# Row vectors, squares and clips of the recurrent tiles on other engines, in a fused transformer kernel

## The reference

```python
# RWKV-7, 4 heads of 64
r, k, v, wd, ad, gd = split_cols(hb)
w_log = -softplus(-(w0 + tanh(wd) @ w_up)) - 0.5
decay = exp(-exp(w_log))
a = sigmoid(a0 + ad @ a_up)
g = sigmoid(gd) @ g_up
kk = l2_normalize(heads(k * k_k), 1e-12)
k = k * (1.0 + (a - 1.0) * k_a)
if v_first is None: v_first = v                                  # layer 0
else: v = v + (v_first - v) * sigmoid(v0 + (v @ v_down) @ v_up)  # layer 1
y = rwkv7_scan(r, decay, k, v, -kk, kk * a)

# gated deltanet, 4 heads of 64, in chunks of 64 tokens
q = l2_normalize(heads(q), 1e-6) * 64 ** -0.5
k = l2_normalize(heads(k), 1e-6)
g = cumsum(g within the chunk)
decay[t, s] = exp(g[t] - g[s]) for s <= t, else 0
```

## Time and profile before

| | |
|---|---|
| three runs | 3709.7, 3712.3, 3714.1 us (median 3712.3) |
| the profiled execution, span | 3708.2 us |
| instructions | 55795 |
| TensorE | busy 3610.1 us |
| VectorE | busy 1972.4 us |
| ScalarE | busy 1502.7 us |
| GpSimd | busy 1623.7 us |
| HBM read | 286 MB |

### The profile page before, as it was taken

One profiled execution on the slowest core, in us unless ns is written; L12 is line 12 of the kernel. 1 busy time (PEld: TensorE's weight loads), 2 busy tenths in 40 slices (PEclk: granted clock), 3 DMA queues, 4 the chain that ended last, 5 costly groups with the idle time before them and its releaser, 6 DMA issues.

```text
span 3708.2 us, 55795 instructions
## 1 busy us (share of the span) xinstructions
PE 3610.1 (97%) x23122; PEld 2996.1 (81%) x23122; DVE 1972.4 (53%) x3453; ACT 1502.7 (41%) x2665; POOL 1623.7 (44%) x883
## 2 busy tenths in 40 slices
PE   9999999999899999999999899999999999999999
PEld 8878888888788888888767888888888866788887
DVE  2356554344645544553677745544652496765552
ACT  3444333434433343333555443334333455534332
POOL 3114566421266635664322135664665322225664
PEclk9999999999999999999999999999999999999999
DMA  4103332311243234322210034323332220012332
GB/s 130 40 29 99 112 103 68 89 52 35 69 136 102 63 101 132 103 63 89 74 46 2 3 125 121 103 66 112 103 102 81 83 57 24 3 42 89 99 103 97
DMA packets 393405, 291.95 MB, mean 79 GB/s; under 512 B 17056, under 2 KB 355904, under 8 KB 393152
## 3 DMA queue, kind: packets, MB, share of 16 engines
q1 hardware_dynamic: 387728, 284.49, 25.2%
q10 hardware_dynamic: 5136, 2.70, 0.4%
q0 software_dynamic: 288, 1.18, 0.1%
HBM read 286.24 MB, written 2.10 MB: 78 GB/s over the span
## 4 chain that ended last, share of the span: by engine, by line
PE 83%; DVE 10%; ACT 4%; issue 1%; POOL 1%; ACTq 0%; DMA 0%; DVEq 0%; SPq 0%; POOLq 0%
PE ps L811 13%; PE ps L812 13%; PE ps L813 13%; PE ps L1040 4%; PE ps L1042 4%; PE ps L1041 4%; PE ps L943 3%; PE ps L940 3%; PE ps L942 3%; PE ps L1068 2%; PE ps L1600 2%; PE ps L1088 2%; PE ps L1077 1%; PE ps L1150 1%; PE ps L838 1%
## 5 line engine op out<-in xcount | busy, mean ns | idle before, releaser
L3453 POOL TENSOR_TENSOR wl<-wraw,wh 128x1024 fp32r<-128x1024 f32 (+1 forms) x424 | 1026.4, 2426 | 1553.1 <-ACT wh L2771 1549.6
L811 PE MATMUL ps<-x_T,wh 128*128 128x512 f32 (+1 forms) x2224 | 850.2, 382 | 0.0
L812 PE MATMUL ps<-x_T,wh 128*128 128x512 f32 (+1 forms) x2224 | 849.0, 382 | 0.0
L813 PE MATMUL ps<-x_T,wl 128*128 128x512 f32 (+1 forms) x2224 | 849.0, 382 | 0.0
L2771 ACT ACTIVATE wh<-wraw 128x1024 fp32r<-128x1024 f32 (+1 forms) x424 | 446.0, 1053 | 763.1 <-PE ps L813 489.1
L811 PEld LDWEIGHTS ps<-x_T,wh 128*128 128x128 f32 x2224 | 418.5, 188 | 81.1 <-issue 0.5
L813 PEld LDWEIGHTS ps<-x_T,wl 128*128 128x128 f32 x2224 | 418.4, 188 | 80.6
L812 PEld LDWEIGHTS ps<-x_T,wh 128*128 128x128 f32 x2224 | 418.4, 188 | 80.7 <-issue 0.5
L2048 DVE TENSOR_TENSOR scr<-scr,ps 128x512 f32<-128x512 f32 x132 | 90.7, 687 | 465.3 <-ACT scr L2926 465.3
L1040 PE MATMUL ps<-wh,h_T 128*128 128x512 f32 x672 | 262.5, 391 | 0.4
L1041 PE MATMUL ps<-wl,h_T 128*128 128x512 f32 x672 | 261.5, 389 | 0.0
(11 more groups left out here) (816 smaller groups left out, 6877.6 us busy)
## 6 DMA issues: line engine op xcount, KB each, us to landing
wraw<-in_ffn_w_gate_dram SPq DMA_DIRECT2D x88, 512.0 KB, 3.9
wraw<-in_ffn_w_up_dram SPq DMA_DIRECT2D x88, 512.0 KB, 3.9
wraw<-in_w_in_dram SPq DMA_DIRECT2D x82, 512.0 KB, 3.8
wraw<-in_w_gate_dram SPq DMA_DIRECT2D x44, 512.0 KB, 3.9
wraw<-in_w_up_dram SPq DMA_DIRECT2D x44, 512.0 KB, 3.8
mix<-in_ffn_w_down_dram SPq DMA_DIRECT2D x20, 1024.0 KB, 7.1
arena<-in_ffn_w_down_dram SPq DMA_DIRECT2D x12, 1024.0 KB, 6.2
wraw<-in_ffn_w_down_dram SPq DMA_DIRECT2D x24, 512.0 KB, 3.7
```

The lines of the kernel that those rows point to most:

```text
L811: mm(b[:, t0:t1], wh[:, k, :], xTh[:, k, t0:t1], k == 0, False)
L812: mm(b[:, t0:t1], wh[:, k, :], xTl[:, k, t0:t1], False, False)
L813: ins = mm(b[:, t0:t1], wl[:, k, :], xTh[:, k, t0:t1], False, k == 7)
L3453: tt(wl, raw_of(w), wh.bitcast(F32), ALU.subtract).then_inc(*g.sig("w", "lo", w))
```

## The change

The row vectors w0, v0 and a0 are no longer added by DVE. PE adds each in the bank, by one more product with K = 1: a row of ones times the row vector. The banks' release moves from DVE's signal "ua" to ACT's "sg", since ACT now takes the Sigmoids right from the banks (in layer 1 three of 256 columns instead of one of 256 and one of 512). The square of kk moves from DVE to ACT, behind the other squares and ahead of the load of the Exp table; DVE signals "kk" for it and later does the sum. The square of q is taken with scale 8, which, with an epsilon of 64e-6, replaces the factor 0.125. The epsilons are added by POOL, from a small tile that five memsets fill at the start. The two clips become two Relu's on ACT, the second with scale -1, and both exponentials get scale -1. The tile eps_o is written but not read.

```diff
--- before.py
+++ after.py
@@ -628,6 +628,7 @@
         ind = con[:, C_IND:C_IND + 2]
         omu = sml(54)[:, 0:7]
         half = sml(55)
+        eps_k, eps_o = sml(56), sml(57)
         vf3 = vfirst[:, :].rearrange("p (t n) -> p t n", t=4)
 
         def c64(n, k=1):
@@ -1459,18 +1460,22 @@
                     ins.then_inc(*S("tin", n))
                 yield
                 KB, BK, tmp = get(), get(), get()
-                b1, f1 = bank(K("lw"), K("ua"))
-                b2, f2 = bank(K("la"), K("ua"))
+                b1, f1 = bank(K("lw"), K("sg"))
+                b2, f2 = bank(K("la"), K("sg"))
                 b3, f3 = bank(K("lg"), K("GG"))
                 pe.wait_ge(*f1)
                 pe.wait_ge(*at("lora", l))
-                ins = mm(b1[:, 0:256], hbT[0:32, 6, js], lora[0:32, :], True, True)
+                pe.wait_ge(*at("pb2", l))
+                mm(b1[:, 0:256], hbT[0:32, 6, js], lora[0:32, :], True, False)
+                ins = mm(b1[:, 0:256], ones[0:1, :], rows["w0"][0:1, :], False, True)
                 if l:
                     pe.wait_ge(*at("rec", "vz", l))
-                    ins = mm(b1[:, 256:512], vz[0:32, js], vup[0:32, :], True, True)
+                    mm(b1[:, 256:512], vz[0:32, js], vup[0:32, :], True, False)
+                    ins = mm(b1[:, 256:512], ones[0:1, :], rows["v0"][0:1, :], False, True)
                 ins.then_inc(*S("b1"))
                 pe.wait_ge(*f2)
-                mm(b2[:, 0:256], hbT[32:64, 6, js], lora[32:64, :], True, True).then_inc(*S("b2"))
+                mm(b2[:, 0:256], hbT[32:64, 6, js], lora[32:64, :], True, False)
+                mm(b2[:, 0:256], ones[32:33, :], rows["a0"][32:33, :], False, True).then_inc(*S("b2"))
                 pe.wait_ge(*f3)
                 mm(b3[:, 0:256], hbT[64:128, 6, js], lora[64:128, :], True, True).then_inc(*S("b3"))
                 yield
@@ -2492,27 +2497,20 @@
                 GG = K3[:, 256:512]
                 yield
                 KB, BK, tmp = get(), get(), get()
-                b1, b2 = psum_of(*K("lw")), psum_of(*K("la"))
-                v.wait_ge(*at(*K("b1")))
-                tt(LW[:, 0:256], b1[:, 0:256], rows["w0"], ALU.add)
-                if l:
-                    tt(UA[:, 256:512], b1[:, 256:512], rows["v0"], ALU.add)
-                v.wait_ge(*at(*K("b2")))
-                tt(UA[:, 0:256], b2[:, 0:256], rows["a0"], ALU.add).then_inc(*S("ua"))
                 yield
                 r_, k_, v_ = RK[:, 0:256], RK[:, 256:512], VV[:, 0:256]
                 a_ = UA[:, 0:256]
                 kk = KB[:, 0:256]
                 nn = sml(j)
                 v.wait_ge(*at(*K("in", 0)))
-                step(tt(kk, k_, rows["k_k"], ALU.mult))
-                step(tt(tmp[:, 0:256], kk, kk, ALU.mult))
-                red(nn[:, 0:4], h64(tmp[:, 0:256], 4), op=ALU.add).then_inc(*S("kk2"))
+                v.wait_ge(*at("pb2", l))
+                tt(kk, k_, rows["k_k"], ALU.mult).then_inc(*S("kk"))
                 yield
                 v.wait_ge(*at(*K("q2")))
-                step(red(nn[:, 4:12], h64(BK, 8), op=ALU.add))
-                ts(nn[:, 0:4], nn[:, 0:4], 1e-12, None, ALU.add)
-                ts(nn[:, 4:12], nn[:, 4:12], 1e-6, None, ALU.add).then_inc(*S("nn"))
+                red(nn[:, 4:12], h64(BK, 8), op=ALU.add)
+                v.wait_ge(*at(*K("kk2")))
+                red(nn[:, 0:4], h64(tmp[:, 0:256], 4), op=ALU.add).then_inc(*S("nn"))
+                v.wait_ge(*v.own())
                 yield
                 v.wait_ge(*at(*K("sg")))
                 step(stt(tmp[:, 0:256], a_, 1.0, rows["k_a"], ALU.subtract, ALU.mult))
@@ -2531,7 +2529,6 @@
                 bcb = bc(gb_[:, j, :].unsqueeze(2), [P, 4, 64])
                 v.wait_ge(*at("rec", "gb", l))
                 v.wait_ge(*at(*K("nroot")))
-                step(ts(nn[:, 4:8], nn[:, 4:8], 0.125, None, ALU.mult))
                 tt(h64(kk, 4), h64(kk, 4), bc(nn[:, 0:4].unsqueeze(2), [P, 4, 64]), ALU.mult)
                 step(tt(h64(QK, 8), h64(QK, 8), bc(nn[:, 4:12].unsqueeze(2), [P, 8, 64]), ALU.mult), *K("QK"))
                 tt(BK[:, 0:256], kk, a_, ALU.mult)
@@ -2567,9 +2564,8 @@
                 RW = [get(), get()]
                 DT, DN = DTN[:, 0:256], DTN[:, 256:512]
                 v.wait_ge(*at(*K("gd")))
-                step(tt(v4(DT), v4(psum_of(*K("gd"))[:, 0:256]), bc(gcs[:, 0:4].unsqueeze(2), [P, 4, 64]), ALU.subtract))
-                step(ts(DN, DT, 0.0, None, ALU.max))
-                ts(DT, DT, 0.0, None, ALU.min).then_inc(*S("DN0"))
+                tt(v4(DT), v4(psum_of(*K("gd"))[:, 0:256]), bc(gcs[:, 0:4].unsqueeze(2), [P, 4, 64]),
+                   ALU.subtract).then_inc(*S("DN0"))
                 yield
                 for par in range(2):
                     if par:
@@ -3232,12 +3228,17 @@
                 nn = sml(j)
                 s.wait_ge(*at("rec", "gg", l))
                 copy(h64(LW[:, 256:512], 4), bc(gg[:, j, :].unsqueeze(2), [P, 4, 64]))
-                s.wait_ge(*at(*K("ua")))
-                act(LW[:, 0:256], LW[:, 0:256], ACT.Sigmoid)
-                w_ = 512 if l else 256
-                act(UA[:, 0:w_], UA[:, 0:w_], ACT.Sigmoid).then_inc(*S("sg"))
+                s.wait_ge(*at(*K("b1")))
+                act(LW[:, 0:256], psum_of(*K("lw"))[:, 0:256], ACT.Sigmoid)
+                if l:
+                    act(UA[:, 256:512], psum_of(*K("lw"))[:, 256:512], ACT.Sigmoid)
+                s.wait_ge(*at(*K("b2")))
+                act(UA[:, 0:256], psum_of(*K("la"))[:, 0:256], ACT.Sigmoid).then_inc(*S("sg"))
                 s.wait_ge(*at(*K("in", 2)))
-                act(BK, QK, ACT.Square).then_inc(*S("q2"))
+                act(BK[:, 0:256], QK[:, 0:256], ACT.Square, scale=8.0)
+                act(BK[:, 256:512], QK[:, 256:512], ACT.Square).then_inc(*S("q2"))
+                s.wait_ge(*at(*K("kk")))
+                act(tmp[:, 0:256], KB[:, 0:256], ACT.Square).then_inc(*S("kk2"))
                 if j:
                     s.preload_act_table(ACT.Exp)
                 yield
@@ -3287,7 +3288,10 @@
                 RW = [get(), get()]
                 yield
                 s.wait_ge(*at(*K("DN0")))
-                act(DTN[:, 0:256], DTN[:, 0:256], ACT.Exp)
+                act(DTN[:, 256:512], DTN[:, 0:256], ACT.Relu).then_inc(*s.sig("step"))
+                s.wait_ge(*s.own())
+                step(act(DTN[:, 0:256], DTN[:, 0:256], ACT.Relu, scale=-1.0))
+                act(DTN[:, 0:256], DTN[:, 0:256], ACT.Exp, scale=-1.0)
                 act(DTN[:, 256:512], DTN[:, 256:512], ACT.Exp, scale=-1.0).then_inc(*S("DN"))
                 if 0 < j < 3:
                     s.preload_act_table(ACT.Sigmoid)
@@ -3492,6 +3496,8 @@
                 yield
                 nn = sml(j)
                 g.wait_ge(*at(*K("nn")))
+                tt(nn[:, 0:12], nn[:, 0:12], eps_k[:, 0:12], ALU.add).then_inc(*S("neps"))
+                g.wait_ge(*g.own())
                 tt(nn[:, 0:12], nn[:, 0:12], half[:, 0:12], ALU.pow).then_inc(*S("nroot"))
                 yield
                 E1, E3X, E4 = get(), get(), get()
@@ -3626,6 +3632,11 @@
                 use(ENDS, True)
                 stage(wat[0] + AHEAD)
 
+            g.memset(eps_k[:, 0:4], 1e-12)
+            g.memset(eps_k[:, 4:8], 64e-6)
+            g.memset(eps_k[:, 8:12], 1e-6)
+            g.memset(eps_o[:, 0:4], 64e-5)
+            g.memset(eps_o[:, 4:8], 1e-6)
             g.memset(half[:, 0:12], -0.5).then_inc(*g.sig("half", 0))
             g.wait_ge(*at("half", 0))
             g.wait_ge(*at("w0", 0))
```

## The result

The changed kernel took 3721.24 us in the median of 7 runs (3717.14 to 3728.70); the kernel before 3711.16 us in 7 runs beside it. The ratio is 1.0026, with a 95% interval of 1.0016 to 1.0035: slower, by 10 us. I had said 3719.9 us, with 0.44 on slower and 0.45 on no measurable difference. The spans of the two profiled executions are 3708.2 and 3719.4 us.

A forecast was written before the change was run, and what follows sets the result against it. In the tiles PE and DVE hand work to each other, neither alone the bound. Layer 0's 2.93 us and layer 1's 4.68 us made +7.6 us on the 3712.3 us median: 3719.9 us, range 3707 to 3729.

The forecast's parts named there:

- The products: Products with ones on PE in each tile's front: +0.63 us in layer 0, +1.06 us in layer 1.
- The square ahead of the table load: ACT squares kk before loading Exp; second solve level in tiles 2 and 3 later by 1.03 us, layer 1 1.46.
- The factor 0.125: DVE's L2534 leaves the path in tiles 2 and 3: -0.20 us in layer 0, -0.35 us in layer 1.
- The clips: L2571 and L2572 leave DVE for two Relu's on ACT; removed time becomes wait: 0, up to 0.25 us.
- The table load's drain: Skill page's drain of about 1380 ns would add some 5.5 us over four tiles; forecast followed the trace, without drain.
- POOL's add: Epsilon add on POOL before the pow: 0.3 us taken, bounds 0.1 and 2.3; on the path in layer 0's tile 1.
- Tile 1: Second tile of each layer: +0.54 us in layer 0, +1.3 us in layer 1, the latter the least certain term.
- Tile 0: First tile of each layer, front beside attention: +0.73 us in layer 0, +1.16 us in layer 1.
- rival C: New idle before the solve's level lowers TensorE's clock, 3.0 us per stretch; 3729 us if three or more tiles; chance 0.14.
- A: DVE is the true bound in the tiles; its removed time, 19 us, comes off: 3693 us; chance 0.09 with half-way forms.
- B: Wait for kk does not bite at the second solve level; idle hides the products: 3710 to 3713 us; chance 0.22.

The follow-up runs named there:

- e1: Kernel before with only the products with ones moved to TensorE: median 3719.3 us, ratio 1.0021, +5.7 us against the kernel before at an equal clock.
- e4: Changed kernel without the products with ones, VectorE adding the row vectors again: 3711.7 us, ratio 0.9996 to the kernel before, -0.4 us at an equal clock.
- e7: Changed kernel with each product with ones issued twice: 3738.4 us, ratio 1.0070 to the kernel before, +16.5 us at an equal clock.
- e8: Kernel before with seven useless products filling TensorE's idle time before L1515 in tiles 2 and 3: 3712.5 us, ratio 1.0001.
- e10: Changed kernel with products of 32 rows of ones instead of one (results wrong, only times used): 3717.1 us, ratio 1.0011 to the kernel before.
- e3: Changed kernel with the Exp table load put ahead of ScalarE's wait for kk and its square: 3723.3 us, ratio 1.0027 to the kernel before.
- e2: Kernel before with only the square of kk on ScalarE, ahead of the Exp table load, its sum moved later: 3712.4 us, ratio 1.0001.

## Why the prediction was right, point by point

**The products: right in kind, too dear in layer 0, and their cover did not exist as an extra.** I took 0.63 and 1.06 us; it is 0.44 (2067.53 - 2066.46 against 0.63) and 0.98 (from 1.06 to 2.04 in layer 1, L1469 at 3241.68 to L1480 at 3243.72). I let the 0.63 us idle swallow the products and then charged the same delay again through the late kk: of the +1.03 us at the second level 0.63 is the products and 0.40 the square. That way of counting hid the main thing: the removal of L2509 and L2510 from before L2645 pays for the wait for ScalarE, and the products are on the path in full. e1 (+5.7), e4 (-0.4) and e7 show that.

**The square ahead of the table load: right in mechanism, mis-sized.** I took 0.40 us for it, beside the products' 0.63. The wait is 0.85 us in all four tiles, but what it adds from kk's start to c1 is 0.15, since the level ran 2.19 us before, beside the end of the u product, and 2.01 now, alone. With the products' 0.44 this is 0.59 against my 1.03; in layer 1 1.13 against 1.46. The slack of 1.3 us in the prediction is that behind the first of the two copies; behind both it was 1.0 (2066.99 + 0.76 = 2067.75, to 2068.76).

**The factor 0.125: right in layer 0, too large in layer 1.** I took 0.20 and 0.35 off. From c1 to PE's next wait for DVE it was 10.90 (2070.95 to 2081.85) and is 10.70 (L1489 at 2080.31 to L1520 at 2091.01): 0.20. In layer 1 it was 0.20 too, not 0.35 (11.07 before, 10.87 after, from 3253.46 to 3264.33):

```profile
2084.24 0.42 DVE L2641 TENSOR_TENSOR arena<-arena,ps 128x256 f32<-128x256 f32 x1 [1.99 <-PE ps L1701]
2084.70 0.43 DVE L2532 TENSOR_TENSOR spare<-spare,small 128x256 f32<-128x256 f32 x1
```

**The clips: right.** They cost and bring nothing. DVE, which had waited 0.66 us in the earlier trace rows, now waits twice, 0.28 and 0.73 us:

```profile
2100.16 0.69 DVE L2575 TENSOR_TENSOR scr<-ps,cr 128x512 f32<-128x512 f32 x1 [0.28 <-PE ps L1566]
2101.59 0.76 DVE L2613 COPY_PREDICATED arena<-cr,ps 128x512 f32<-128x512 int32 x1 [0.73 <-PE ps L1605]
```

**The table load's drain.** By the Trainium skill ("ScalarE: Activation LUTs", What ACT_TABLE_LOAD costs) a switch of tables costs a drain of about 1380 ns on top of the load. In the changed kernel the copy starts at 2077.86, 0.01 us after the load's end at 2077.85. The row decides. An estimate by the page's figure would have put the sum about 5.5 us higher than the forecast.

**POOL's add: right.** I took 0.3 with its wait; L3499 lasts 0.21 and the power starts 0.29 us after it in tile 1, 0.36 and 0.44 in tile 3.

```profile
2008.28 0.21 POOL L3499 TENSOR_TENSOR small<-small 128x12 f32<-128x12 f32 x1 [40.28 <-DVE small L2512]
2008.57 2.27 POOL L3501 TENSOR_TENSOR small<-small 128x12 f32<-128x12 f32 x1
```

**Tile 1: right in layer 0.** 37.65 to 38.23 us at full clock, +0.58 against my 0.54 (the products alone 0.36 in e1, all the rest 0.22 in e4); in layer 1 39.14 to 40.15, +1.01 against 1.3.

**Tile 0: too dear in layer 0.** I took +0.73 us. From the attention product (L1077, L1078) that waits 0.34 us shortly ahead of this front to the tile's first mask copy, e8, which has the kernel before's tile 0, and e10 have windows at full clock:

```profile
1941.26:1984.68 43.42, 42.37 (x308) 30.43 (x308) 32.28 (x111) 26.83 (x74) 9.23 (x8) 1.00 0.00 1
1938.77:1982.34 43.57, 42.83 (x312) 30.85 (x312) 29.79 (x103) 28.00 (x78) 9.67 (x9) 1.00 0.00 1
```

It is +0.15 (43.59 in e3, +0.17). In layer 1 no version with products has this tile at full clock to its end; from its first low-rank product to attention's L1088 (L1089 in e10), still at full clock, it is +1.43 us (16.23 in e10, 3111.54 to 3127.77, against 14.80, 3110.80 to 3125.60), and how much of that remains at the end is open. My term was 1.16.

**The sum.** At full clock: tiles 2 and 3 of layer 0 +0.39 each (37.99 in e10 against 37.60 in e8; forecast 0.83), of layer 1 +0.92 (39.11 against 38.19; forecast 1.11), tile 1 +0.58 and +1.01, together 4.2. Tile 0 of layer 0 adds 0.15, and tile 0 of layer 1 something up to 1.4, so the sum is 4.4 to 5.8. The forecast was 7.6. At an equal clock the runs say 6.5 +- 1.4.

**The clock made up the rest.** The difference of the means is 8.9 us, 3721.8 less 3712.9 (10.1 by the medians); 2.5 of it go with a mean clock of 0.9891 against 0.9904. In the profiled execution tiles 2 and 3 of layer 0 took 41.06 and 41.05 us at a clock of 0.92, about 3.0 us more than in e10, which is rival C's price. Tiles 1 to 3 of both layers together took 240.72 us there against 232.10 in the profile of the kernel before; 4.2 of these 8.6 us are there at full clock too, the rest is half clock. The stretch in tile 3 of layer 0:

```profile
2064.73:2105.78 41.05, 36.79 (x835) 33.06 (x836) 29.50 (x61) 17.23 (x46) 10.13 (x9) 0.92 0.01 3
2068.00:2074.00 6.00, 6.00 (x104) 5.52 (x103) 0.81 (x2) 2.21 (x7) 0.00 (x0) 0.50 0.00 1
```

But C's reason, the idle time before the level, is not borne out: the stretch of tile 3 is over before that wait (2078.30), and so is that of tile 2 (2027 to 2034; its wait, the first of the layer, ends at 2037.24). e2 and e4 with the same wait ran at 0.9917 and 0.9910. So the total came out near partly by luck: a sum that was 1 to 3 us too high and a clock effect of 2.5 us that I had not put in. Whether the lower clock belongs to the change is open. The versions with products of one row had 0.9891, 0.9895, 0.9879, 0.9905 and, twice, 0.9860; those without 0.9895 to 0.9917, so one by one they overlap. Taken together, the 42 runs with such products average 0.9890 and the 178 without any 0.9905, apart by 0.0015 +- 0.0006 (0.0011 without e7). So the lower clock seems to go with the products, but what in them would bring it about no run shows. Two readings of mine on the clock were also wrong: the 38.0 us that I took for a tile of layer 0 held a stretch itself (at full clock it is 37.6), and of the four tiles 2 and 3 before, three had one (0.96, 0.95 and 0.92), not one.

**The rivals.** A (VectorE is the bound) fell with e1, where two additions less per tile in layer 0 and three in layer 1 brought nothing. B (the wait for kk does not bite) was wrong because of the products, which the idle time did not hide; for all the rest it came near, as e4 shows, though the wait was there.

## What to carry to other kernels

Where an instruction is moved to an engine that is in step with another, ask first what stands behind it there: here a table load of 1.28 us stood behind a wait that it did not need, and putting it ahead made 1.1 us per tile out of a change that had brought nothing. The same edit at a place where the operand is already there costs 1.2 us (tile 1 of e3), so such an order is chosen place by place. Work taken off VectorE pays only where TensorE waits for it, and a small product on the engine that holds 83% of the chain was paid in full in tiles 2 and 3 (0.36 us of 0.44 in tile 1 of layer 0, in e1).
